# A two-block transformer kernel: first stage and last layer norm reworked, splits of weights moved behind a block's last tile

## What is computed

```python
def first_block(x, ...):                       # DEPTH = 1
    hn = rmsnorm(h, mix_norm_pre)              # h = x
    z, xbc, dt_raw, u = split(hn @ w_in)
    mix = concat(ssd_mixer(z, xbc, dt_raw, ...), pool_mixer(u, ...)) @ w_out
    h = h + rmsnorm(mix, mix_norm_post)
    h = h + rmsnorm(conv_glu(rmsnorm(h, ...), w_ffn_up, ..., w_ffn_down), ...)
    gate = sigmoid(rmsnorm(h, ple_norm_pre) @ w_ple_gate)
    return h + rmsnorm(gate * (p @ w_ple), ple_norm_post)

def second_block(x, ...):
    h = layer_norm(ALPHA * h + fox_branch(h, ...), ln_gain[0], ln_bias[0])
    h = layer_norm(ALPHA * h + retention_branch(h, ...), ln_gain[1], ln_bias[1])

def layer_norm(x, g, b):
    return (x - mean(x)) * rsqrt(var(x) + LN_EPS) * g + b
```

## Time and profile before

| | us |
|---|---|
| median of 3 runs | 2412.04 (2411.9 to 2412.15) |
| the profiled execution, whole | 2410.22 |
| its span (first to last instruction) | 2408.4 |
| TensorE busy | 2367.5 |
| VectorE busy | 1526.0 |
| ScalarE busy | 1200.8 |
| GpSimd busy | 290.8 |

### The profile page before, as it was taken

One profiled execution on the slowest core, in us unless ns is written; L12 is line 12 of the kernel. 1 busy time (PEld: TensorE's weight loads), 2 busy tenths in 40 slices (PEclk: granted clock), 3 DMA queues, 4 the chain that ended last, 5 costly groups with the idle time before them and its releaser, 6 DMA issues.

```text
span 2408.4 us, 29790 instructions
## 1 busy us (share of the span) xinstructions
PE 2367.5 (98%) x11868; PEld 1981.9 (82%) x11868; DVE 1526.0 (63%) x1954; ACT 1200.8 (50%) x1612; POOL 290.8 (12%) x272
## 2 busy tenths in 40 slices
PE   7999999999999999999999999999999999999997
PEld 6778888888888888888788888887888888888886
DVE  6898578765457766575755556656665654656556
ACT  6767464444444444464655555544444443444442
POOL 4163003321012231000000000001000000000001
PEclk9999999999999999999999999999999999999999
DMA  6445656665666666655556565564655756566653
GB/s 241 139 140 176 226 180 191 188 190 192 193 192 189 187 192 209 193 193 184 169 182 203 165 185 158 165 192 132 207 179 178 227 182 197 179 179 183 187 179 118
DMA packets 123323, 441.92 MB, mean 183 GB/s; under 512 B 13488, under 2 KB 17072, under 8 KB 122672
## 3 DMA queue, kind: packets, MB, share of 16 engines
q1 hardware_dynamic: 123184, 440.02, 58.3%
HBM read 437.87 MB, written 2.10 MB: 183 GB/s over the span
## 4 chain that ended last, share of the span: by engine, by line
PE 93%; DVE 3%; ACT 2%; POOL 1%; DMA 1%; issue 0%; SPq 0%; POOLq 0%; DVEq 0%; ACTq 0%
PE bank L672 92%; DVE wlo L1460 1%; DVE ev L1463 1%; POOL acc L2099 1%; ACT whi L1012 1%; DVE S L1463 0%; DVE hn L1463 0%; PE bank L763 0%; DMA raw<-in_w 0%; PE bank L1003 0%; PE bank L936 0%; PE bank L958 0%; DMA hT<-in_xT 0%; DVE xa L1460 0%; ACT S L1119 0%
## 5 line engine op out<-in xcount | busy, mean ns | idle before, releaser
L1460 DVE TENSOR_TENSOR wlo<-raw,whi 128x1024 fp32r<-128x1024 f32 x808 | 1013.7, 1258 | 779.3 <-ACT whi L1012 777.3
L1012 ACT ACTIVATE whi<-raw 128x1024 fp32r<-128x1024 f32 (+1 forms) x810 | 854.3, 1057 | 962.7 <-PE bank L672 947.9
L672 PE MATMUL bank<-xa,whi 128*128 128x512 f32 (+1 forms) x2688 | 844.6, 396 | 13.3 <-DVE wlo L1460 10.7
L672 PE MATMUL bank<-whi,xa 128*128 128x512 f32 x2048 | 641.5, 395 | 2.8 <-DVE wlo L1460 2.6
L672 PEld LDWEIGHTS bank<-xa,wlo 128*128 128x128 f32 x2656 | 499.0, 189 | 114.8
L672 PE MATMUL bank<-xa,wlo 128*128 128x256 f32 (+1 forms) x2656 | 522.8, 278 | 0.0
L672 PE MATMUL bank<-whi,xb 128*128 128x512 f32 x1536 | 475.0, 391 | 0.0
L672 PEld LDWEIGHTS bank<-whi,xa 128*128 128x128 f32 x2048 | 379.1, 188 | 85.4 <-issue 6.9
L672 PEld LDWEIGHTS bank<-xa,whi 128*128 128x128 f32 x2688 | 411.7, 189 | 23.5 <-DVE wlo L1460 10.7
L672 PE MATMUL bank<-wlo,xa 128*128 128x512 f32 x1024 | 399.8, 390 | 0.0
L672 PEld LDWEIGHTS bank<-whi,xb 128*128 128x128 f32 x1536 | 287.9, 188 | 59.4 <-DVE wlo L1460 0.2
(11 more groups left out here) (238 smaller groups left out, 1281.2 us busy)
## 6 DMA issues: line engine op xcount, KB each, us to landing
raw<-in_w SPq DMA_DIRECT2D x804, 512.0 KB, 3.6
hT<-in_ln_rows SPq DMA_DIRECT2D x2, 2048.0 KB, 8.8
X<-in_post SPq DMA_DIRECT2D x3, 768.0 KB, 5.4
hT<-in_xT SPq DMA_DIRECT2D x4, 512.0 KB, 7.8
hT<-in_x SPq DMA_DIRECT2D x1, 2048.0 KB, 8.1
out<-S SPq DMA_DIRECT2D x8, 256.0 KB, 2.5
X<-in_dec SPq DMA_DIRECT2D x8, 192.0 KB, 4.8
raw<-in_w SPq DMA_DIRECT2D x5, 256.0 KB, 2.5
```

The source lines that it names most:

```text
L672: return pe.matmul(o, w, x, start=start, stop=stop, skip_group_check=True)
L1012: act.activation(hi, r, ACT.Copy).then_inc(*w_high(i))
L1460: return dve.tensor_tensor(o, x, y, op)
```

## The change

**The start.** `STARTS` cuts the first block's pieces into 1, 1, 2, 4, 4 and 4 k tiles, and x with them, so the first block has six pieces instead of four and all later numbers rise by two. Only 16 columns of `par` come ahead; the rest, and 256 columns of `con`, come behind x, the other 1280 later. ScalarE does a root on a spare column first; TensorE does four matmuls on zeros first. The sum of squares now comes from x in its natural layout (tokens on partitions), which is loaded in quarters to S1 between weight pieces: ScalarE squares with a sum (`x_squares`, at pieces 0 to 3), `x_factor` at piece 5 and `x_row` at piece 10 turn it into the row `rs`.

**Splits.** HELD and HELD_BACK get three more entries, and the calls move as the diff shows. **The last norm.** `lead` is 1 in the last block; the quads of t = 1 are multiplied by the gain ahead of the factor (`by_gain`), TensorE makes b + diag(shift) g in PSUM, and one VectorE instruction per quad ends it; ScalarE and GpSimd do none. Also, the exponential of a_log moves ahead of the delta logarithm. The diff, cut, in the order of the file: `layout`, the constants, TensorE's program, ScalarE's, VectorE's.

```diff
+STARTS = [(0, 1), (1, 1), (2, 2), (4, 4), (8, 4), (12, 4)]
...
-    squares_of_x(0)
-    late(11, "load_counts")
+    for i in range(4):
+        late(i, "x_squares", i)
+    late(5, "x_factor")
+    late(6, "hot")
+    late(10, "x_row")
+    late(2, "load_con")
+    late(13, "load_counts")
-    conv_at = {8: (6, (0, 3, 5)), 10: (4, (0, 3, 5))}
...
-        e = block("conv", c, xa0, "w_in", col, full)
-        d, cuts = conv_at.get(c, (1, (0, 3, 5)))
+        e = block("conv", c, xa0, "w_in", col, STARTS if c == 8 else full)
+        d, cuts = {8: 5, 10: 3}.get(c, 1), (0, 3, 5)
...
-                                            2, {} if half else None)
+                                            2, {} if half else None, 4, 1)
...
-        HELD = (LAST - 2, LAST - 1, LAST, LAST + 1)
-        HELD_BACK = HELD + (MIX - 2, MIX - 1, MIX) + (GATE - 2, GATE - 1, GATE, GATE + 1)
+        HELD = (LAST - 3, LAST - 2, LAST - 1, LAST, LAST + 1, LAST + 3)
+        HELD_BACK = HELD + (MIX - 2, MIX - 1, MIX) + (GATE - 3, GATE - 2, GATE - 1, GATE, GATE + 1)
...
+            q.wait_ge(*vec_val.of("zeros"))
+            for _ in range(4):
+                mm(bank[7][:, 0:T], rs[:, 0:128], rs[:, :], True, True)
...
+                    elif step == "layer_norm" and k[0]:
+                        q.wait_ge(rows_in, 32)
+                        for c in range(4):
...
+                            mm(bank[4 + c][:, :], ident, rowb[:, 512 * c:512 * c + 512], True)
+                        q.wait_ge(*vec_val.of("diagonal"))
+                        for c in range(4):
+                            mm(bank[4 + c][:, :], diagonal, rowg[:, 512 * c:512 * c + 512], False,
+                               True).then_inc(*side("ln_row", c))
...
+                    elif step == "x_row":
+                        q.wait_ge(*vec_val.of("rsn"))
                         q.wait_ge(con_in, 16)
                         for t in range(2):
+                            m = mm(bank[4][:, 128 * t:128 * t + 128], rsn[:, t:t + 1].broadcast_to((128, 128)), ident,
+                                   t == 0, t == 1)
...
+                if what == "dt":
+                    act.activation(A[:, 0:32], pc("a_log", 0, 32), ACT.Exp).then_inc(*act_val("ea"))
                 q.wait_ge(*vec_val.of(what, "one_plus"))
                 act.activation(v[2], v[1], ACT.Ln).then_inc(*act_val(what, "ln"))
...
+                    elif step == "x_squares":
+                        i, = k
+                        q.wait_ge(xn_in[i], 16)
+                        t = i // 2
+                        for c in (2 * (i % 2), 2 * (i % 2) + 1):
+                            square_sum(sn[:, t, 512 * c:512 * c + 512], ss[:, t, c:c + 1], "x", t, c)
...
+                    elif step == "x_row":
+                        q.wait_ge(*side.of("x_row"))
+                        act.activation(rs[:, :], bank[4][:, 0:T], ACT.Copy).then_inc(*act_evac("x_row"))
...
                             rms_root(2, 0)
+                            split(GATE - 3 + AHEAD)
                             act.activation(sm[:, 389:390], eps5, ACT.Sigmoid)
+                            split(GATE - 2 + AHEAD)
                             rms_high(2, 0)
-                            split(GATE - 2 + AHEAD)
...
                         root(l, 0)
                         if l == 0:
+                            split(HELD[0] + AHEAD)
                             center(2)
                             center(5)
                             quad_high(0)
-                            split(HELD[0] + AHEAD)
+                            split(HELD[1] + AHEAD)
...
                     elif step == "low_quads":
                         i, = k
+                        if i == 6:
+                            split(HELD[5] + AHEAD)
                         quad_high(i)
...
                         else:
                             q.wait_ge(rows_in, 32)
+                            for c in range(3):
+                                last_gain(0, c)
+                                if c == 0:
+                                    invert(1, 0)
+                                last_bias(0, c)
+                            add_out(1, 1, 3, n + 1)
+                            aggregate(1, 1)
+                            by_gain(3)
+                            invert(1, 1)
+                            q.wait_ge(*vec_val.now())
+                            ts(diagonal, ident, ln_b[:, 1:2], None, ALU.mult).then_inc(*vec_val("diagonal"))
+                            last_gain(0, 3)
+                            last_bias(0, 3)
+                            for c in range(4):
+                                x = sn[:, 1, 512 * c:512 * c + 512]
+                                q.wait_ge(*vec_val.of("by_gain", c))
+                                q.wait_ge(*side.of("ln_row", c))
+                                stt(x, x, ln_f[:, 1:2], bank[4 + c][:, :], ALU.mult, ALU.add).then_inc(*vec_val("out", 1, c))
```

More of the change, by code:

```diff
@@ L455, in block_kernel @@
         raw_in = [semaphore(f"raw{i}") for i in range(NRAW)]
-        x_in = [semaphore(f"x{i}") for i in range(4)]
+        x_in = [semaphore(f"x{i}") for i in range(len(STARTS))]
+        xn_in = [semaphore(f"xn{i}") for i in range(4)]
+        pre_in, tables_in = semaphore("pre"), semaphore("tables")
         decay_in = [semaphore(f"decay{i}") for i in range(2)]
@@ L1103, in scalar_program @@
                     if step == "start":
[L1104 to L1111 removed]
+                        q.wait_ge(*vec_val.of("eps"))
@@ new lines, in scalar_program @@
+                        act.activation(spare, eps5, ACT.Sqrt)
+                        q.wait_ge(pre_in, 16)
+                        for i, (k0, n) in enumerate(STARTS):
+                            q.wait_ge(x_in[i], 16)
+                            for j in range(k0, k0 + n):
+                                act.activation(xa[:, j, 0:T], hT[:, j, :], ACT.Copy,
+                                               scale=pc("mix_pre", j)).then_inc(*x_high("xa", 0, j))
+                            if i < AHEAD:
+                                split(i)
+                    elif step == "hot":
@@ L1976, in vector_program @@
                             add_out(int(step == "ret_out1"), t, k[0].arg, k[0].tile + t)
+                        if step == "ret_out1":
+                            by_gain(k[0].arg)
                     elif step == "layer_norm":
@@ L2027, in vector_program @@
                             bias(i + 1)
+                            split(HELD[5] + AHEAD)
+                        quad_low(i)
                     elif step in ("rq", "rk"):
@@ L2196, in pool_program @@
                         m.then_inc(*pool_val("late_gain"))
-                    elif step == "layer_norm" and k[0]:
-                        q.wait_ge(rows_in, 32)
-                        for t, c in BY_POOL:
-                            x = sn[:, t, 512 * c:512 * c + 512]
-                            q.wait_ge(*act_val.of("centered", 1, t, c))
-                            tt(x, x, rowg[:, 512 * c:512 * c + 512], ALU.mult).then_inc(*pool_val("scaled", t, c))
-                            q.wait_ge(*pool_val.now())
-                            tt(x, x, rowb[:, 512 * c:512 * c + 512], ALU.add).then_inc(*pool_val("out", t, c))
                     elif step in ("rq", "rk"):
```

160 lines of the change are left out of this document (64 added, 96 removed).

## The result

| | before | changed |
|---|---|---|
| median, us | 2412.10 (2411.9 to 2412.66, 4 runs) | 2396.32 (2395.19 to 2397.04, 4 runs) |
| the profiled execution, whole | 2410.22 | 2397.04 |
| its span | 2408.4 | 2395.3 |

The ratio is 0.9934, with a 95% interval from 0.9917 to 0.9951: 15.8 us by the medians (11.8 to 20.0 by the interval), 13.2 by the two profiled executions. The forecast was 2392.0 with a range of 2387.5 to 2399; it said 20 us. The sign and the range held, the likeliest case did not. The changed kernel was run twice more beside the experiments: 2395.34 (5 runs, ratio 0.9936) and 2395.57 (5 runs, 0.9938).

A forecast was written before the change was run, and what follows sets the result against it. TensorE was taken as the bound, busy 2367.5 of 2408.4 us, leaving its stands and lost clock. Start and convolution stage 12, splits 5.5 and last norm 2.3 summed to 19.8 us, forecasting 2392 (range 2387.5 to 2399).

The forecast's parts named there:

- The two stands of the first block: First block: TensorE would stand some 3 us ahead of piece 3 and 1.6 us ahead of piece 2.
- 7.1 for the start: Start: smaller first pieces and no stand for GpSimd's sum of squares, nor its low clock, gain 7.1 us.
- 5 for the stage: Convolution stage, 50 to 94 us: VectorE's chain starts earlier, its lag shrinks about 4 us; 5 of 6.1 us taken.
- So 2.5 us are sure here: First block's end: TensorE ends it at 21.2 instead of 23.7 us; 3.2 gained if transfers run a tenth faster.
- If VectorE still ran late at 80: Convolution stage: a stated sign that the prediction was wrong, VectorE still late at 80 us.
- The splits: Fox and gate blocks: splits moved behind the last tile remove stands of 1.94 and 1.41 us; 5.5 us taken.
- its clock: Fox block: the low clock (0.58 for 3.66 us) behind the 1.94 us stand goes too, 1.5 us.
- (a): Convolution stage takes the gain back because VectorE sets its end: 7 instead of 12 us, 2397; chance 0.20.
- (b): Fox and gate blocks: moved splits make the next pieces late, 0.5 instead of 5.5 us, 2397; chance 0.10.
- (e): Start changes nothing, stands only move, and the tail's matmuls eat its gain: 2410; chance 0.02.
- (d): Start: squares hold back the splits of pieces 6 to 9, slower than before, 2421; chance 0.03.
- (c): Start: clock stays up through short pieces and transfers run at 400 GB/s, 1.5 + 1.5 us more, 2389; chance 0.10.

The follow-up runs named there:

- s12: The changed kernel itself, measured again beside three follow-up runs, against the kernel before: 2395.57 us, ratio 0.9938.
- s8: The changed kernel itself, measured again beside three other follow-up runs, against the kernel before: 2395.34 us, ratio 0.9936.
- s4: The changed kernel without the four matmuls on zeros at its start: 2395.82 us, ratio 0.9938 to the kernel before.
- s5: The changed kernel with the row of factors, scaling and taps of the first two convolution blocks one piece earlier: 2394.85 us, ratio 0.9934 to the kernel before.
- s6: The changed kernel without loading or squaring natural x (sum of squares a constant, output not the reference's): 2394.19 us, ratio 0.9931 to the kernel before.
- s7: The changed kernel with row, scaling and first two blocks' taps and the partial squares' sum a piece earlier, small constant copies at piece 11: 2394.55 us, ratio 0.9931.
- s10: The changed kernel with the third and fourth transposes of the convolution's output one piece later: 2392.78 us, ratio 0.9926 to the kernel before.
- s1: The changed kernel with the splits at the fox and gate blocks placed as before: 2401.13 us, ratio 0.9962 to the kernel before.
- s3: The changed kernel's new start alone, with splits and last norm as before: 2404.33 us, ratio 0.9972 to the kernel before.
- s9: The changed kernel with twelve VectorE convolution taps on 32 instead of 256 columns (output not the reference's): 2392.67 us, ratio 0.9924 to the kernel before.

## Why the prediction was right, and where it failed

**Right.** The first matmul at 5.0 (4.80). The two stands of the first block: 1.6 and 3 forecast, 2.64 and 1.17 in this trace, 1.33 and 2.95 in s12, so it is about their sum (4.6; 3.8, 4.3 and, in s8, 4.8) that was foretold and not the split, which goes with the clock between them. No stand at 40. The zeros buy 0.4 at most (nothing, s4). The last norm 2.3 (2.4). The gate stand of 1.41 went, and of the 1.4 us 1.0 stayed, since a wait of 1.09 us for VectorE took its place at 1148.93.

**What failed: 12 us for the start and the stage.** They gave 6.8. Two terms of the sum were wrong, 7.1 for the start (measured 5.1, at 46.84) and 5 for the stage (measured 1.7, the rest up to 87.61).

**The start, 7.1 against 5.1.** "So 2.5 us are sure here": at the end of the first block, by the start of the next, the lead was -0.2. The forecast had the block end at 21.2, thus piece 3 begin at 12.9 (12 k tiles of 0.695 earlier); it began at 13.94, and the next stand was 1.39 and not 1.0. In s8, where the clock stayed up to 14.4, piece 3 began at 13.21 and the clock fell behind it. In the thirteen traces with the new start piece 3 began at 12.9 to 14.5. What was right is the stand for GpSimd (3.2) and the low clock behind it; the recorded sum takes that clock as 2.0 us in one place ("as if at 46.6") and as 1.7 in another, since 46.6 less 39.2 would be 7.4.

**The stage, 5 against 1.7: the step that failed.** "VectorE's lag shrinks by about 4 us, more than any single wait of the stage", hence 5 of the 6.1 us to be had there. No wait came off: TensorE's stands were 4.6 us before (0.59, 1.41, 0.61, 2.04) and 4.8 after (1.91, 0.90, 2.04). The 1.7 us are the low clock (0.96 over 43.84 us) that one of those stands was followed by in the trace of before. And the lead fell from 5.1 to 3.8 us at the first wait for VectorE. "If VectorE still ran late at 80" was one of the prediction's own signs of being wrong, and it came: 0.90 us at 78.31. Two numbers of the chain were wrong.

- *VectorE's start.* I had the row of factors at 36.5 to 37.3 and the chain at 39.5. TensorE's small matmuls for the row ran at 38.03, where the forecast's own sum has 36.1 (39.2 less 2.78 and 0.36), so 2 of the 5 us were lost already there. The row was there at 40.6, because ScalarE's copy of it stood behind a split that waited for its raw piece, and the chain began at 44.54, behind one more split that waited for its raw piece:

```profile
39.23 1.06 ACT L1036 ACTIVATE whi<-raw 128x1024 fp32r<-128x1024 f32 x1 [1.61 <-DMA raw<-in_w]
40.19 0.37 ACT L1157 ACTIVATE rs<-bank 128x256 f32<-128x256 f32 x1
42.26 1.06 ACT L1036 ACTIVATE whi<-raw 128x1024 fp32r<-128x1024 f32 x1 [1.71 <-DMA raw<-in_w]
...
43.36 1.26 DVE L1486 TENSOR_TENSOR wlo<-raw,whi 128x1024 fp32r<-128x1024 f32 x1 [1.81 <-ACT whi L1036]
```

  Such a piece is asked for once VectorE has freed its buffer, and VectorE was late: at 20 to 30 it was busy for only 3.68 of 10 us, since ScalarE squared and waited for natural x (2.15 us at 20.37), and then for 8.8 of 10 up to 40. The piece of the second wait was asked for at 37.44, as VectorE ended a split, and took 4.8 us to land, where the one before took 3.5. In the first wait the DMA engines moved 155 GB/s (36 to 38), so it was not for bandwidth; in the second 369 (40 to 42), near the 409 of 20 to 30, so there bandwidth may have a share. That link was read from the code and the trace, no run tests it. s5 showed that placing the taps earlier does not help while that lasts. Against s8's 43.25 the chain began 1.7 us earlier without the squares (s6), where TensorE's row then held it, and 1.8 us earlier without ScalarE's rest of 1.55 us and the small copies and in the earlier place (s7). The two were not tried together, so whether 39.5 can be reached stays open.
- *Its length.* 38.2 us of work and "some 3" of waits for others made 41 to 41.5. It is 43.1, as it had been (43.84): 38.9 of work and 4.2 of waits. The number stood in the trace of before and I did not measure it from tap to end. The 2.0 us wait for ScalarE of the earlier trace rows was counted among the waits that would go with VectorE's lag; it is set by the order inside one piece (s10).

The chain's end was to be 39.5 + 41.5 = 81 and was 44.5 + 43.1 = 87.6, 6.6 us late; the forecast had kept 1.4 of that in hand (94.4 less 81 is 13.4, and it took 12), which leaves the 5.2 us that are missing.

**The clock behind it.** Another 1.5 us went behind the 2.04 us stand in this profiled execution, where the kernel before had kept its clock. In s8 it was kept. So it is not in every execution of the changed kernel, but it is most of why two profiles of one kernel differ by 2.5 us. That the medians (15.8) show more than the two profiles (13.2) comes mostly from the other side: the profiled execution of before was 1.9 us below its median, that of the changed kernel 0.7 above.

**The splits.** Mechanism and size right, 4.5 + 1.0 for 5.5. But 1.5 of my terms was "its clock": behind the same stand it held in s1 and in s3 (1.93 us, 1.00 both). That term is one that some executions have and others have not; the stand itself and the later wait of 1.22 us, both back in s1, are the sure part.

**Rivals.** (a), with 0.20, has the mechanism: VectorE sets the end of the stage (s9), and early pieces did not shorten its work. That its 7 us fit as well is luck: it took the 7.1 of the start and nothing from the stage, and measured are 5.1 and 1.7. That the whole came out inside the range goes with it. (b) and (e) are refuted by s1 and s3, (d) by the result; (c) did not occur, and s8, with the clock up through the short pieces, shows that this alone gives 0.7 us at k tile 17.

## What to carry to other kernels

An earlier first matmul is not yet a gain: compare the same matmul one block later, since here 5.9 us were gone by the second block. When work is pulled ahead of a stage, measure the stage in the old trace from its first dependent instruction to its end on the engine that does most of it, and ask when that engine can start, with all that its queue still holds; if the length is as long as that engine's work plus its round trips, an earlier start is all that can be won. Sort each wait in the stage by what it takes to end it: some go with the lag, but a wait on another engine's copy inside the same step stays until the order is changed, and such a change of one number gave more here (2.8 us) than any of three changes of the start (0.5, 0.8 and 1.2). A saving that rests on the clock recovering after a stand is worth its chance, not its full price.

## What the runs showed of the hardware

**The same stand, with and without a fall of the clock.** In the fourteen traces, at the convolution stage and the two turned blocks, there are 18 stands of TensorE of 1.81 to 2.10 us. In the 3 us that follow (from 0.5 us on) the granted clock was 0.50 to 0.63 behind nine of them and 1.00 behind the other nine, with the same instructions at the same place; a stand of 2.78 us (s5) was followed by 1.00. Of 46 stands of 0.88 to 1.41 us one was followed by a low clock (74.20 in the kernel before, 0.72). By place, the clock fell in six of eight at ScalarE's copy (2.02 to 2.04 us), in two of seven at the wait for X near 52 (1.81 to 2.10) and in one of three at the fox block (1.93, 1.94); whether the place matters, so few cannot tell. A fall costs 1.4 to 1.7 us here. So a stand near 2 us had in these runs about even odds to cost nearly double, and one of 1.4 or less hardly any. The Trainium skill (TensorE: Matmul & The Clock Gate, Part 1, What's actually happening) calls the ramp variable from run to run, because what the chip looks at runs freely of the kernel; the pairs above, s8 against the changed kernel and s1 against before, agree.

**VectorE beside GpSimd.** Four taps took 2.15 or 2.62 us while GpSimd scaled, 1.66 alone; in the last norm a product took 1.11 against 0.73. The Trainium skill (GPSIMD Engine Reference, 8. Key points) says that GpSimd shares its SBUF interfaces with VectorE and contends with instructions that have two SBUF inputs; both rows are of that kind and agree.

**fp32 matmuls.** Eight passes of 512 columns took 3.60 us twice, 0.45 each; as forecast from the six at 2220.
